# A top-k search over two tiles: GpSimd moves each tile's threshold by itself

## The reference

```python
logits = jnp.einsum('bqhd,bsd->bqhs', qib, k_idx).astype(jnp.float32) * IDX_SCALE
score = jnp.einsum('bqh,bqhs->bqs', wb.astype(jnp.float32), jax.nn.relu(logits))
causal = key_pos[None, :] <= tq[:, None]
score = jnp.where(causal[None], score, -jnp.inf)
_, sel = lax.top_k(score, n_keep)          # n_keep = 256
```

## Time and profile before

| | us |
|---|---|
| median of 3 runs (lowest, highest) | 3409.25 (3407.23, 3410.01) |
| the profiled execution, its own time | 3407.94 |
| its span, first to last instruction | 3406.1 |
| PE, DVE, ACT, POOL busy in the span | 3075.7, 1694.6, 1332.1, 328.1 |
| granted clock of TensorE over the span | 0.94 |

### The profile page before, as it was taken

The page is one execution under the profiler, slowest core; times in us unless marked ns, Lnnn a source line. Parts: engine busy times, 40 slices in busy tenths (PEclk is TensorE's granted clock), DMA queues, the critical chain, the costliest instruction groups (busy, mean ns, idle before and its releaser), DMA issues.

```text
span 3406.1 us, 37933 instructions
## 1 busy us (share of the span) xinstructions
PE 3075.7 (90%) x13944; PEld 2364.1 (69%) x13944; DVE 1694.6 (50%) x3385; ACT 1332.1 (39%) x2162; POOL 328.1 (10%) x421
## 2 busy tenths in 40 slices
PE   5998887788887888997899999999999999999998
PEld 4776765566666666785688856888668886588873
DVE  3376767677876767731333343333433334333333
ACT  3253436566756557653323222322222223232221
POOL 1332320213030130000000000000000000000000
PEclk9998987888997888998999999999999999999999
DMA  3111122221110110101633312323213323132310
GB/s 121 55 46 51 41 84 71 57 57 44 37 50 27 44 34 20 53 30 50 231 99 97 119 51 75 117 94 99 87 57 124 99 87 105 50 121 90 99 50 25
DMA packets 215452, 250.88 MB, mean 74 GB/s; under 512 B 57952, under 2 KB 160096, under 8 KB 215264
## 3 DMA queue, kind: packets, MB, share of 16 engines
q1 hardware_dynamic: 212960, 239.99, 22.2%
q10 hardware_dynamic: 2304, 8.39, 0.6%
...
## 4 chain that ended last, share of the span: by engine, by line
issue 60%; PE 23%; DVE 8%; ACT 5%; POOL 2%; DMA 1%; SPq 0%; DVEq 0%; POOLq 0%; ACTq 0%
PE bank L1673 6%; PE bank L1653 5%; PE bank L1538 5%; PE bank L1556 2%; PE bank L1639 2%; PE bank L1557 2%; ACT kept L895 1%; DVE kept L1199 1%; ACT score_tail L895 1%; POOL score L816 1%; DVE too_few L1207 1%; ACT probsT L983 1%; DVE probs L1328 1%; POOL rstdC L840 1%; DVE threshold L1216 1%
## 5 line engine op out<-in xcount | busy, mean ns | idle before, releaser
L1403 DVE TENSOR_TENSOR w_lo<-w_raw,w_hi 128x1024 fp32r<-128x1024 f32 x256 | 312.6, 1222 | 517.5 <-ACT w_hi L1026 511.3
L1026 ACT CAST w_hi<-w_raw 128x1024 fp32r<-128x1024 f32 x256 | 267.3, 1045 | 561.7 <-PE bank L1538 535.1
L1653 PE MATMUL bank<-values,probsT 128*128 128x64 f32 x2176 | 333.2, 300 | 144.8 <-ACT probsT L983 120.8
L1653 PEld LDWEIGHTS bank<-values,probsT 128*128 128x128 f32 x2176 | 312.1, 218 | 171.5 <-ACT probsT L983 159.4
L1538 PE MATMUL bank<-hn_hi,w_hi 128*128 128x512 f32 x1024 | 399.8, 390 | 14.5 <-DVE hn_lo L1420 10.8
L1538 PE MATMUL bank<-w_hi,hid_lo 128*128 128x512 f32 x1024 | 405.9, 396 | 0.0
L1538 PE MATMUL bank<-w_lo,hid_hi 128*128 128x512 f32 x1024 | 405.9, 396 | 0.0
L1538 PE MATMUL bank<-w_hi,hid_hi 128*128 128x512 f32 x1024 | 405.9, 396 | 0.0
L1538 PE MATMUL bank<-hn_lo,w_hi 128*128 128x512 f32 x1024 | 399.2, 390 | 0.0
L1538 PE MATMUL bank<-hn_hi,w_lo 128*128 128x512 f32 x1024 | 399.2, 390 | 0.0
L1328 DVE CUSTOM_DVE_ANT_0 probs<-bank,mask 128x384 f32<-128x384 f32 (+3 forms) x320 | 193.9, 607 | 248.1 <-PE bank L1557 247.4
...
## 6 DMA issues: line engine op xcount, KB each, us to landing
...
```

Source lines behind the costliest of these rows:

```text
L1026: nc.scalar.copy(w_hi[:, p % 4, :].rearrange("p (k f) -> p k f", f=piece_width(p)), raw_piece(p)).then_inc(w_hi_rdy, 1)
L1403: nc.vector.tensor_tensor(out_p, raw_piece(p), hi_p.bitcast(F32), ALU.subtract).then_inc(w_lo_rdy, 1)
L1653: last = nc.tensor.matmul(bank[:, 4, h * HEAD:(h + 1) * HEAD], probsT[:, m % 3, a * P:(a + 1) * P], values[:, kt, HEAD * kv:HEAD * (kv + 1 ...
```

## The change

From pair 6 on (`t >= EARLY_PICKS`), VectorE no longer moves the thresholds. GpSimd does, tile by tile: `move_threshold(t, k)` in its stream waits for VectorE's count (`exact_count`), moves the even tile's threshold and signals `level[0]`, for which VectorE's next count waits; then it waits for ScalarE's count (`act_count`), moves the odd tile's and signals `level[1]`, for which ScalarE's next count waits. The thresholds move by signed half steps: `half` is halved each round, `fewer` is 0 or −2, `change` is (fewer + 1) × half, so that the threshold goes up or down by half; the last round only goes down or stays. A round other than the first is eight GpSimd instructions of 128x1. `pending` is used for pairs 2 and 4 alone.

The planner's condition changes too: no round of pair 6 is early any more, so that the late list has 160 rounds in place of 152, over the same 244 steps. The rounds of pairs 6 to 14 lie in steps 0 to 20, 30 to 58, 74 to 103, 127 to 163 and 185 to 229 (before: 0 to 16, 27 to 53, 71 to 99, 124 to 161, 184 to 229). 17 of these steps hold two rounds; before, 18 late steps held two or three. In GpSimd's stream `mean_root` and `add_residual` now stand ahead of the step's search part.

```diff
             t = args[0]
-            if kind in ("settle", "toggle", "pick") and t >= EARLY_PICKS or t >= EARLY_PICKS + 2:
+            if kind in ("round", "settle", "toggle", "pick") and t >= EARLY_PICKS:
                 break
...
+        def levels(t):
+
+            return (ROUNDS + 1) * (t // 2 - EARLY_PICKS // 2)
...
+            def move_threshold(t, k):
+
+                if k == 0:
+                    for c in range(2):
+                        pool.wait_ge((exact_count, act_count)[c], ROUNDS * (t // 2 - 1))
+                        if t >= FIRST_PICK + 2:
+                            pool.wait_ge(dropped, t - FIRST_PICK)
+                        nc.gpsimd.memset(threshold[:, c:c + 1], 0).then_inc(level[c], 1)
+                else:
+                    for c in range(2):
+                        own = slice(c, c + 1)
+                        nc.gpsimd.tensor_scalar(half[:, own], half[:, own], 0.5, None, ALU.mult).then_inc(level_step[c], 1)
+                for c in range(2):
+                    own = slice(c, c + 1)
+                    done = 3 * (ROUNDS * (t // 2 - EARLY_PICKS // 2) + k)
+                    pool.wait_ge((exact_count, act_count)[c], ROUNDS * (t // 2 - 1) + k + 1)
+                    nc.gpsimd.tensor_scalar(fewer[:, own], below[:, own], float(P * (t + 2) - 2 * KEEP), -2.0,
+                                            ALU.is_gt, ALU.mult).then_inc(level_step[c], 1)
+                    if k == 0:
+                        pool.wait_ge(level_step[c], done + 1)
+                        nc.gpsimd.tensor_scalar(half[:, own], fewer[:, own], 1.0, float(1 << 30), ALU.add,
+                                                ALU.mult).then_inc(level_step[c], 1)
+                        nc.gpsimd.tensor_scalar(flip[:, own], fewer[:, own], 0.5, None, ALU.mult).then_inc(level_step[c], 1)
+                        pool.wait_ge(level_step[c], done + 3)
+                        nc.gpsimd.tensor_copy(change[:, own], half[:, own]).then_inc(turned[c], 1)
+                        pool.wait_ge(turned[c], t // 2 - EARLY_PICKS // 2 + 1)
+                        nc.gpsimd.tensor_tensor(threshold[:, own], change[:, own], flip[:, own], ALU.add).then_inc(level[c], 1)
+                    else:
+                        pool.wait_ge(level_step[c], done + 2)
+                        nc.gpsimd.tensor_scalar(change[:, own], fewer[:, own], 1.0, half[:, own],
+                                                ALU.add if k < ROUNDS - 1 else ALU.mult, ALU.mult).then_inc(level_step[c], 1)
+                        pool.wait_ge(level_step[c], done + 3)
+                        nc.gpsimd.tensor_tensor(threshold[:, own], threshold[:, own], change[:, own],
+                                                ALU.add).then_inc(level[c], 1)
+
             def spread_mask(t, dropping):
...
             def search_part(spot, dropping):
+                for t, k in at["round"].get(spot, ()):
+                    if t >= EARLY_PICKS:
+                        move_threshold(t, k)
                 for (t,) in at["toggle"].get(spot, ()):
...
                 i, h = divmod(H, Q_HEADS)
-                search_part(EARLY_SPOTS + m, late_drop)
                 if b == 0 and h == 7 and i >= 1:
...
                     add_residual(i - 1)
+                search_part(EARLY_SPOTS + m, late_drop)
                 sum_heads(at["index"].get(EARLY_SPOTS + m, ()))
...
-                act.wait_ge(thr_rdy, tries(t) + k + 1)
+                if t < EARLY_PICKS:
+                    act.wait_ge(thr_rdy, tries(t) + k + 1)
+                else:
+                    act.wait_ge(level[1], levels(t) + k + 1)
                 if k == 0:
...
-                dve.wait_ge(thr_rdy, tries(t) + k + 1)
-                if k > 0:
+                if t < EARLY_PICKS:
+                    dve.wait_ge(thr_rdy, tries(t) + k + 1)
+                else:
+                    dve.wait_ge(level[0], levels(t) + k + 1)
+                    if k == 0:
+                        dve.wait_ge(score_rdy, t - FIRST_PICK + 1)
+                if k > 0 and t < EARLY_PICKS:
                     nc.vector.tensor_scalar(next_tried[:], threshold[:], 2 ** (31 - k) // 2, None,
...
-                dve.wait_ge(thr_rdy, tries(t) + ROUNDS + 1)
+                if t < EARLY_PICKS:
+                    dve.wait_ge(thr_rdy, tries(t) + ROUNDS + 1)
+                else:
+                    dve.wait_ge(level[1], levels(t) + ROUNDS + 1)
                 nc.vector.tensor_scalar(junk[:, 0:P * (t + 1)], score_of(t), threshold[:, 1:2].bitcast(F32), 0.0,
...
                         dve.wait_ge(raised, t // 2)
+                    elif t < EARLY_PICKS:
+                        dve.wait_ge(thr_rdy, tries(t) + ROUNDS + 1)
                     else:
-                        dve.wait_ge(thr_rdy, tries(t) + ROUNDS + 1)
+                        dve.wait_ge(level[0], levels(t) + ROUNDS + 1)
                     nc.vector.tensor_scalar(junk[:, 0:keys], x, limit, 0.0, ALU.is_gt, ALU.add,
...
                     move_pending()
-                    if k == 0:
+                    if k == 0 and t < EARLY_PICKS:
                         start_search(t)
                     count_exact(t, k, junk)
-                    pending.append((t, k))
+                    if t < EARLY_PICKS:
+                        pending.append((t, k))
                 for (t,) in at["settle"].get(spot, ()):
```

6 lines of the change are left out of this document (added).

## The result

| | us |
|---|---|
| before, median of 4 runs (lowest, highest) | 3409.63 (3407.23, 3410.07) |
| changed, median of 4 runs (lowest, highest) | 3476.18 (3468.22, 3479.55) |
| ratio, 95% interval | 1.0194 [1.0182, 1.0206] |
| the profiled execution, its own time; its span | 3479.55; 3477.4 |
| granted clock of TensorE over the span | 0.931 |

The change makes the kernel 66.6 us slower. I had forecast 47 us faster, and the time lies outside the range.

The account below looks back on a forecast made before the run. The prediction took the attention stage's search rounds to be bound by waits between engines, no engine being full. From 3407.9 us, −20 −70 +20 +11 +14 −1 = −46 gave 3362 us, range 3303 to 3430.

Parts of the forecast that it names:

- VectorE's three instructions, −20: Late rounds: removing VectorE's three small instructions, 76.8 us busy, saves a quarter, 20 us (bounds 0 and −77).
- ScalarE no longer waits, −70: Late rounds: of ScalarE's 93.1 us waiting for thresholds moved behind the mask, a quarter stays; −70 us.
- the mask's detour: VectorE's threshold move stands behind the next step's mask, which waits for PE; ScalarE's 93.1 us of waits at stake.
- What GpSimd costs: GpSimd's moves: 0.20 us an instruction, one half 0.83 us, both 1.7; nothing added in steps with one round.
- the circle: Scores, mask, counts, moves, copy, weighing over three steps: some 7.8 us, 2.6 a step, under the 3.92 of before.
- the sign of a wrong cover: The cover is wrong if VectorE waits for GpSimd's threshold by more than 0.2 us a round.
- Two rounds in a step, +20: 17 steps with two rounds: ScalarE waits 1.7 us instead of 0.5 between them; +20 us.
- Root and residual, +11: GpSimd's mean root and residual add delay moves or wait behind them in 8 tiles; +11 us (bounds 0 and +30).
- Eight rounds of pair 6, +14 −1: Eight rounds leaving the last projection tile save 1 us there and cost 1.8 each late, +14 us.
- The second: Rival: GpSimd becomes the search's clock, from about 0.5 us an instruction; +63 us, 3471; chance 0.15.
- The third, "the wait only moves": Rival: ScalarE's mask wait becomes an equally long one for VectorE's count plus two halves; 3400 to 3430; chance 0.20.
- wrong in the circle if ScalarE's total wait stays over 80 us at a price of 0.20: Stated failure sign: ScalarE's total threshold wait over 80 us though GpSimd's one-column instructions take 0.20 us.

Follow-up runs that it names:

- e8_own: e3_short, but VectorE moves its own column right behind its count and GpSimd moves ScalarE's alone; 3393.08 us.
- e3_short: e2_swap with two values prepared while the counts run, so each half of the move is a chain of two instructions, not three; 3401.13 us.
- e2_swap: The changed kernel with the two halves swapped in GpSimd's stream, ScalarE's threshold moved first; 3410.96 us.
- e6_count_first: e2_swap with VectorE's first count of a step placed ahead of the step's masks; 3431.89 us.
- e14_long_v: e2_swap with two dependent spare GpSimd instructions (0.6 us) in VectorE's half of the move; 3438.91 us.
- e13_own_tied: e8_own with ScalarE's half of the move waiting for VectorE's count too; 3421.78 us.
- e1_plan: The kernel before with the new planner condition and root and residual ahead of GpSimd's search part; VectorE still moves thresholds; 3419.60 us.
- e15_long_s: e2_swap with two dependent spare GpSimd instructions (0.6 us) in ScalarE's half of the move; 3466.58 us.
- e4_joint: The changed kernel with one GpSimd move for both columns behind both counts, five instructions a round instead of eight; 3467.26 us.
- e10_tied: e2_swap with both counts waited for ahead of each half of the move; 3495.63 us.
- e9_long: The changed kernel with one more dependent one-column GpSimd instruction in each half of the move; 3511.27 us.
- e12_own_early: e8_own with the planner's condition of the kernel before, rounds 0 to 7 of pair 6 early again; 3384.51 us.
- e7_move_first: The kernel before with VectorE's threshold move ahead of a step's masks instead of behind them; 3381.95 us.
- e11_dve_extra: The kernel before with three spare 128x2 VectorE instructions behind each late count; 3424.57 us.

## Why the prediction was wrong

**The waits of the two searches.** For every kernel I took from the timelines of the late rounds the mean time from the end of VectorE's count to the start of ScalarE's next one, and from the tables of waits (500 to 1500 us) what ScalarE's count waited for moved thresholds and what VectorE waited for a moved threshold or, where it moves both itself, for ScalarE's count. The first twelve have 160 late rounds, the last four 152. Least wait of ScalarE first:

| kernel | us from VectorE's end to ScalarE's start | ScalarE waits | VectorE waits | median |
|---|---|---|---|---|
| e8_own | 1.58 | 47.0 | 0 | 3393.08 |
| e3_short | 1.23 | 57.1 | 61.4 | 3401.13 |
| e2_swap | 1.16 | 65.9 | 86.9 | 3410.96 |
| e6_count_first | 2.11 | 70.7 | 177.7 | 3431.89 |
| e14_long_v | 0.85 | 82.6 | 140.6 | 3438.91 |
| e13_own_tied | 2.17 | 85.5 | 0 | 3421.78 |
| e1_plan | 1.93 | 89.3 | 8.8 | 3419.60 |
| e15_long_s | 1.57 | 116.8 | 133.2 | 3466.58 |
| e4_joint | 2.19 | 125.1 | 93.8 | 3467.26 |
| e10_tied | 1.73 | 135.4 | 144.1 | 3495.63 |
| changed | 2.85 | 135.9 | 43.8 | 3476.18 |
| e9_long | 3.32 | 171.8 | 67.2 | 3511.27 |
| e12_own_early | 1.54 | 49.3 | 0 | 3384.51 |
| e7_move_first | 1.45 | 72.1 | 18.3 | 3381.95 |
| before | 1.99 | 93.1 | 5.7 | 3409.63 |
| e11_dve_extra | 2.06 | 109.5 | 3.7 | 3424.57 |

Among the twelve the time goes with ScalarE's wait: from e8_own to e9_long the wait grows by 125 us and the time by 118. VectorE's wait counts for less: the changed kernel and e10_tied have the same wait of ScalarE, e10_tied has 100 us more of VectorE's and is 19 us slower. The way from VectorE's end to ScalarE's start alone does not sort the kernels (e10_tied has 1.73 us of it and is slower than the changed kernel), but it says how the changed kernel came to its wait: ScalarE's next count starts 2.85 us behind VectorE's, not 1.99. Moving the threshold out of the mask's shadow put it behind VectorE's half of the move, and that is longer. ScalarE's count and readout then end 0.33 us *after* VectorE's on average, where before they ended 0.28 ahead, and the copy for which PE waits stands behind them.

**One round in a step and two.** The timelines also part the loss by steps. This is the mean time from one start of ScalarE's count to the next, with a copy between the two (another step) and back to back (the same step), with the number of cases:

| kernel | another step | same step |
|---|---|---|
| e1_plan | 4.04 (138) | 2.09 (17) |
| changed | 4.30 (138) | 3.26 (17) |
| e2_swap | 3.90 (138) | 2.58 (17) |

e1_plan has the order of rounds of the changed kernel and differs in who moves. Between the two lie 138 × 0.26 = 36 us and 17 × 1.17 = 20 us, together the 56 us that e1_plan left open. e2_swap is 19 us under e1_plan in the first kind and 8 over it in the second.

**By the steps of the sum:**

- *VectorE's three instructions, −20.* About −13 (e11_dve_extra).
- *ScalarE no longer waits, −70.* Wrong in size and sign: the wait rose to 135.9 us. I had written that ScalarE's half is moved only after VectorE's, and still left only a quarter; it fails with the next step, which had that wait as covered. e7_move_first shows what the mask's detour was worth by itself: 27 us, with ScalarE's wait shorter by 21. The other 72 us of the wait stayed with the count that the move stands behind.
- *What GpSimd costs; "So in steps with one round: nothing".* **This is the step that failed.** Its price held: 1.00 us a half with both hand-overs, against my 0.83 without the last. What failed is the circle: in steps with one round the moves cost not nothing but the 36 us above, and that against a kernel that still has the detour. I laid the parts over three steps, got 2.6 us a step, under the 3.92 there were, and called the difference slack. But the slack is a mean over a circle whose parts wait one for the other in every round, and where rounds follow closely there was none: VectorE waited 43.8 us for a move that I had as covered but for 0.1 us a round (it was 0.27, over the 0.2 that I had set as the sign of a wrong cover), and every extra microsecond of a hop cost 0.3 of one (e14_long_v) to 0.6 (e15_long_s), measured at the engine that it delays most.
- *Two rounds in a step, +20.* Right, against e1_plan with its same order: 17 × 1.17 = 20 us.
- *Root and residual, +11.* Not run by itself in the changed kernel, and part of the 36 us; it stays open.
- *Eight rounds of pair 6, +14 −1.* Together +11 measured (e1_plan), 9 in e12_own_early. The last projection tile did shrink, from 24.80 to 23.64 us, but that hardly reached the attention: its first mask starts at 496.18 us, before at 496.24.

The −13 and the +11 nearly cancel, so the +67 is the cost of hop and order (if the parts add; e10_tied and e13_own_tied say that they do so only roughly). Order is the larger: 65 us go with the two halves swapped. Of the two waits that ScalarE had, the one for VectorE's count weighs more: in e4_joint and e10_tied ScalarE has this one alone, and the first saves 9 us, the second loses 19. Both also delay VectorE, so no run gives each wait a price of its own.

**By the rivals.** The second, GpSimd as the clock of the search, gave 3471, within 6 us of the result, and is wrong all the same: its condition was 0.5 us an instruction and GpSimd full. The rows show 0.19 to 0.26 and GpSimd busy 47% of the round stretches. e4_joint, with three instructions fewer, and e2_swap, with the same number, confirm that its load doesn't matter. The third, "the wait only moves", was the mechanism. Its size was too small, as it let the wait keep its length; it ended at 3430. The sentence on record "wrong in the circle if ScalarE's total wait stays over 80 us at a price of 0.20" is what happened.

**By the rule.** The rows show GpSimd's 128x1 instructions at 188 to 264 ns; VectorE's own 128x1 ones in e8_own take 148 to 184. I had called the two alike; GpSimd's compare takes 227 ns against VectorE's 154. The Trainium skill (Perfetto Trace Analysis, Optimizing GPSIMD Operations) says to prefer other engines wherever possible. By that rule the change had to lose, and it did, but the speed of the engine is the smaller part: e2_swap has the same instructions on GpSimd and costs nothing, and e8_own and e12_own_early have ScalarE's threshold moved by GpSimd and are faster than before. The lowest median, e7_move_first's, does without GpSimd, but e12_own_early is level with it.
